# The inner layer of the compression on column strips: sixteen positions of a half go in turn to four strips of 32 columns

## The reference, cut to what matters

```python
def compress(kv, pos_emb, w1, b1, w2):       # kv: (1, 256, 2 groups, 128)
    n_cmp = (S - 32) // 16 + 1               # 15 windows
    idx = arange(n_cmp)[:, None] * 16 + arange(32)[None, :]
    blocks = kv[:, idx] + pos_emb            # (15 windows, 32 positions, 2 groups, 128)
    flat = blocks.reshape(n_cmp, G, 32 * 128)
    return silu(flat @ w1 + b1) @ w2         # w1: (4096, 128), w2: (128, 128)
```

## Time and profile before

| what | value |
|---|---|
| median of three runs | 2127.25 us |
| the profiled execution | 2127.4 us |
| its span on the core | 2125.6 us |
| TensorE matmul busy | 2095.3 us (99% of the span), 11559 records |
| TensorE weight loads busy | 1799.6 us (85%) |
| VectorE / ScalarE / GpSimd busy | 1413.3 / 1050.3 / 106.2 us |
| share of TensorE in the chain that ended last | 79% |
| mean granted TensorE clock | 0.999 |

### The profile page before, as it was taken

How to read it: one execution, slowest core, us unless ns; L and a number is a source line. 1 busy time by engine, 2 the same in 40 slices (tenths; PEclk the granted TensorE clock), 3 DMA queues, 4 the chain that set the end, 5 groups by cost and what they waited for, 6 DMA issues and landing times.

```text
span 2125.6 us, 27729 instructions
## 1 busy us (share of the span) xinstructions
PE 2095.3 (99%) x11559; PEld 1799.6 (85%) x11559; DVE 1413.3 (66%) x1802; ACT 1050.3 (49%) x1520; POOL 106.2 (5%) x121
## 2 busy tenths in 40 slices
PE   8999999999999999999999999999999999999998
PEld 7989888989888888887888888888888878888887
DVE  5657876657877766665675566675766667655655
ACT  5344646444645555545454454554544454444543
POOL 0100010010010010000000000000100000000000
PEclk9999999999999999999999999999999999999999
DMA  8353245453235665444554465565644545544552
GB/s 284 112 199 128 94 136 180 122 199 125 95 123 203 209 217 172 164 139 159 178 181 157 149 216 189 198 208 184 212 156 159 158 159 178 184 173 151 194 184 96
DMA packets 193271, 357.24 MB, mean 168 GB/s; under 512 B 8381, under 2 KB 85369, under 8 KB 193146
## 3 DMA queue, kind: packets, MB, share of 16 engines
q1 hardware_dynamic: 190410, 345.51, 48.7%
q0 software_dynamic: 2736, 9.96, 1.3%
HBM read 354.40 MB, written 1.05 MB: 167 GB/s over the span
## 4 chain that ended last, share of the span: by engine, by line
PE 79%; DVE 3%; ACT 1%; issue 0%; DMA 0%; POOL 0%; DVEq 0%; ACTq 0%
PE bank L2029 14%; PE bank L2033 14%; PE bank L2039 14%; PE bank L2071 12%; PE bank L2075 6%; PE bank L2093 2%; PE bank L2084 2%; PE bank L2053 2%; PE bank L2056 2%; PE bank L2059 2%; PE bank L2110 1%; PE bank L2213 1%; DVE raw_r L2538 1%; PE bank L2101 1%; PE bank L2296 1%; PE bank L2131 1%
## 5 line engine op out<-in xcount | busy, mean ns | idle before, releaser
L2538 DVE TENSOR_TENSOR raw_r<-raw,high 128x2048 fp32r<-128x2048 f32 x304 | 686.3, 2267 | 78.4 <-ACT high L2322 77.2
L2322 ACT ACTIVATE high<-raw 128x2048 fp32r<-128x2048 f32 x304 | 575.5, 1897 | 228.2 <-PE bank L2039 173.0
L2029 PE MATMUL bank<-high,units_r 128*128 128x512 f32 (+1 forms) x1576 | 628.8, 399 | 4.4 <-ACT high L2322 3.0
L2033 PE MATMUL bank<-high,units_r 128*128 128x512 f32 (+1 forms) x1576 | 615.3, 390 | 2.0 <-DVE units_r L2562 1.1
L2039 PE MATMUL bank<-raw_r,units_r 128*128 128x512 f32 (+1 forms) x1576 | 423.4, 389 | 0.0
L2029 PEld LDWEIGHTS bank<-high,units_r 128*128 128x128 f32 x1576 | 296.8, 188 | 65.5 <-issue 4.0
L2033 PEld LDWEIGHTS bank<-high,units_r 128*128 128x128 f32 x1576 | 297.0, 188 | 61.3 <-DVE units_r L2559 2.2
L2039 PEld LDWEIGHTS bank<-raw_r,units_r 128*128 128x128 f32 x1576 | 296.1, 188 | 62.3 <-DVE raw_r L2538 0.7
L2071 PE MATMUL bank<-units_r,high 128*128 128x512 f32 x1152 | 288.2, 392 | 0.0
L2071 PEld LDWEIGHTS bank<-units_r,high 128*128 128x128 f32 x1152 | 208.4, 189 | 38.1
L2075 PEld LDWEIGHTS bank<-units_r,raw_r 128*128 128x128 f32 x1152 | 157.2, 190 | 11.2
(11 more groups left out here) (262 smaller groups left out, 2207.2 us busy)
## 6 DMA issues: line engine op xcount, KB each, us to landing
raw<-in_ffn_w_dram SPq DMA_DIRECT2D x132, 1024.0 KB, 5.1
raw<-in_w_in_dram SPq DMA_DIRECT2D x108, 1024.0 KB, 5.1
raw<-in_w_out_dram SPq DMA_DIRECT2D x24, 1024.0 KB, 4.9
raw<-in_cross_wkv_dram SPq DMA_DIRECT2D x16, 1024.0 KB, 5.2
raw<-in_w_branch_dram SPq DMA_DIRECT2D x12, 1024.0 KB, 4.9
raw<-in_cross_wq_dram SPq DMA_DIRECT2D x8, 1024.0 KB, 5.4
raw<-in_cross_wo_dram SPq DMA_DIRECT2D x8, 1024.0 KB, 4.9
raw<-in_w_in_dram SPq DMA_DIRECT2D x4, 832.0 KB, 4.5
```

The costliest lines, as they stand in the source:

```text
L2029: pe.matmul(o, h.high(k0 + k)[:, span], p.hi[k][:, cols], start=start and k == 0, stop=False, skip_group_check=True)
L2033: pe.matmul(o, h.low(k0 + k)[:, span], p.hi[k][:, cols], start=False, stop=False, skip_group_check=True)
L2322: done = act.activation(high, raw, ACT.Copy)
L2538: done = dve.tensor_tensor(low, raw, high.bitcast(F32), ALU.subtract)
```

## The change

The rows of e4 are padded from 15 to 16 windows per group, so that one position has 32 columns; the padding is set to zero by a memset. The 16 matmuls of a half write in turn to PSUM partitions 0 to 31, 32 to 63, 64 to 95 and 96 to 127, so each of the four strips collects eight of the 32 positions. The copy out takes all 128 partitions, and the turn is no longer a transpose: it multiplies the copied tile with a constant `sum4` (128 x 32, ones where the row modulo 32 is the column), which turns and adds the four strips at once. The step's entry in `plan.work` falls from 16 x 512 to 16 x 170 per half.

```diff
+    put("sum4", (p % 32 == j)[:, 0:32])
...
-                e4 = e.ap[:, 0:960].rearrange("p (l g n) -> p l g n", l=32, g=2)
+                e4 = e.ap.rearrange("p (l g n) -> p l g n", l=32, g=2)
...
-                    plan.work += 16 * 512
+                    plan.work += 16 * 170
...
-                hb, hs = st(30), st(30)
+                hb, hs = st(32), st(32)
...
-                c = plan.copy(f"{C}.hp", [("cmp_1", C)], hp.ap[0:30, 0:P], b.ap[0:30, 0:P], "dve", hp.after)
+                c = plan.copy(f"{C}.hp", [("cmp_1", C)], hp.ap[:, 0:P], b.ap[:, 0:P], "dve", hp.after)
...
         for i in range(16):
-            product = pe.matmul(bank.ap[0:30, 0:P], e4[:, 16 * half + i, :, :].rearrange("p g n -> p (g n)"),
-                                p.raw[:, i * P:i * P + P], start=half + i == 0, stop=half + i == 16,
+            strip = i % 4 * 32
+            product = pe.matmul(bank.ap[strip:strip + 32, 0:P], e4[:, 16 * half + i, :, :].rearrange("p g n -> p (g n)"),
+                                p.raw[:, i * P:i * P + P], start=half == 0 and i < 4, stop=half == 1 and i >= 12,
                                 skip_group_check=True)
...
-        pe.transpose(bank.ap[:, 0:30], src[0:30, 0:P], ident[0:30, 0:30]).then_inc(
+        hold.wait_ge(*at(("const",)))
+        pe.matmul(bank.ap[:, 0:32], src[:, 0:P], m.cst("sum4"), start=True, stop=True, skip_group_check=True).then_inc(
...
-            product = pe.matmul(bank.ap[0:15, g * P:g * P + P], hs[:, g * 15:g * 15 + 15], p.raw, start=True, stop=True,
+            product = pe.matmul(bank.ap[0:15, g * P:g * P + P], hs[:, g * 16:g * 16 + 15], p.raw, start=True, stop=True,
...
+        dve.memset(e4[:, :, :, 15:16], 0.0)
...
-                done = dve.tensor_tensor(e4[:, 16 * half:16 * half + 16, g, :], blocks[:, :, half:half + 15],
+                done = dve.tensor_tensor(e4[:, 16 * half:16 * half + 16, g, 0:15], blocks[:, :, half:half + 15],
...
-        dve.tensor_scalar(hb, bank.ap[:, 0:30], bias, None, ALU.add).then_inc(*mark(s.vout, ("cmp_bias", name)))
+        dve.tensor_scalar(hb, bank.ap[:, 0:32], bias, None, ALU.add).then_inc(*mark(s.vout, ("cmp_bias", name)))
```

## The result

| | before | changed | ratio (95% interval) |
|---|---|---|---|
| median of four runs each | 2126.80 us | 2107.72 us | 0.9911 (0.9899 to 0.9924) |
| range of the runs | 2126.23 to 2131.13 | 2107.38 to 2108.62 | |
| the profiled execution / its span | 2127.4 / 2125.6 | 2107.87 / 2106.1 | |

The change takes 19 us off, 0.9%. The forecast was 2115.2 us with a range from 2109.0: the direction was right, the saving was over half as large again as said, and it lies outside the range. It is close to the rival called full overlap (2109.7).

The account below looks back on a forecast made before the run. TensorE, busy in 99% of the span, was taken as the bound. From 2127.4 us: compressions -13.6, turns +0.4, switches +0.65, waits for the w1 piece +0.35, together -12.2, giving 2115.2 us; range 2109 to 2128.5.

Parts of the forecast that it names:

- full overlap: Rival for the four compression stretches: all strips work at once, 0.0275 to 0.037 us a record, 2109.7 to 2111.5 us; chance 0.28.
- The second record of instruction i can't start until the first has left the strip, and instruction i+1 stands behind it.: Compression matmuls: only neighbouring instructions overlap, so 32 take 33 record times, 3.62 us for 7.03; 13.6 us saved in four.
- The Trainium skill's order rule: Compression matmuls: starts and ends strictly in program order, taken as speaking against reading the skill's 3.07x into this change.
- Bounds: One compression's 64 records: 7.03 us without overlap, 1.76 with four strips at once; a 32-column load estimated at some 27 ns.
- The switches, +0.65 us in eight: TensorE going from whole array to strips and back: between 0 and 1.3 us in all, the middle taken.
- The turn, +0.4: The turn as a two-record float32 product instead of one record: +0.1 us each, +0.4 in four.
- Small edits, nothing: Memsets, strided additions, copy out, bias with 32 columns and 16 KB more constants: no cost; without cover 0.6 us a layer.
- The wait for the second piece of w1: Between the halves of the values' compression TensorE waits for the load: 0.1 and 0.2 us, put down as +0.35 in all.
- pairs: Main case for the compressions: only an instruction's second record and the next one's first overlap, 3.62 us each, 2115.2 us; chance 0.42.
- VectorE's waits: Sign to look for: VectorE's four waits for the compression, 6.2 us each, fall to about 2.8 each.
- What would come late next: After the values' compression: next w_in piece ready 12 us before use, TensorE's 1.95 us wait for VectorE stays, saving kept.
- The clock, which was left out: Granted clock 1.00 in the compression stretches and TensorE busy on both sides, so no clock term was counted.

## Why the prediction was wrong

Step by step, as it was put:

- **"The second record of instruction i can't start until the first has left the strip, and instruction i+1 stands behind it."** This is the step that failed. The first half of the sentence holds; the second doesn't. Instruction i+1 goes to another strip's queue, and the row that would have priced it was not there. A compression took 1.88 us where 3.62 was said, without the waits for the piece. Four of them are 7.0 us. That this is nearly the whole miss of 7.5 us is in part luck: the waits for the piece were 2.6 us dearer than said, and turns, switches and start-up came out cheaper by 0.9, 0.65 and 1.4. I had taken the order in which records start in the trace of before as a rule of the engine; there all records of a stretch like this use the same columns, so that order could not show what other columns do. The runs for eight, six, four and two records in a row fix what holds instead: order of handing out, four places per strip.
- **The Trainium skill's order rule.** On that step I had leaned on "TensorE: Matmul & The Clock Gate", Part 3, Packing small matmuls, which says that matmuls start and end strictly in program order. The trace disagrees for column strips: with eight records in a row the ninth starts with the fifth, ahead of the sixth to the eighth, and in turn, where each float32 instruction is two records, four strips start at once and full overlap is nearly reached, 7.10 / 1.88 = 3.8x. Its 3.07x for four row tiles is lower than what column strips give here. The measurement decides.
- **Bounds.** The two ends, 1.76 and 7.03 us, were right, and nothing speaks against the estimate of 27 ns for a load of 32 columns: no load held up a matmul (64 records in 1.88 us are 29 ns each). The full overlap's end of the range was set at 2109 from 2109.7, without room for its own small terms being too dear: 1.05 us were put down for turns and switches, and they came to -0.5.
- **The switches, +0.65 us in eight.** Nothing. "The trace has no such switch" was a misreading: the kernel before pays on the way into these products and out of them, as much as the changed one. The way in, before and then after:

```profile
93.72 1.07 PE L2039 MATMUL bank<-raw_r,units_r 128*128 128x512 f32 x4
94.72 7.17 PE L2131 MATMUL bank<-raw,units 128*30 128x128 f32 x64
...
92.26 1.07 PE L2040 MATMUL bank<-raw_r,units_r 128*128 128x512 f32 x4
```

  It is 1.00 us from the first of four products to the compression in both (92.26 to 93.26 after), 0.09 more than to a turn from 128 partitions. On the way out, 7.10 - 64 x 0.109 = 0.12 us are left before and 1.88 - 16 x 0.109 = 0.14 after. "TensorEngine Tiling (Array Packing)", Key Properties, in the Trainium skill says that a change of mode drains TensorE. No run here shows whether the kernel before changes the mode for its 30 columns too; with the 1.3 us that I worked out for the rule the sum would have been 1.3 too high.
- **The turn, +0.4.** It is -0.5: 0.13 us each against 0.17 to the next start, and 0.09 less ahead of each. The rows of 15 x 15 and 128 x 15 were poor neighbours.
- **Small edits, nothing.** Right within the interval: 0.9997 (0.9988 to 1.0007) with all of them and no strips.
- **The wait for the second piece of w1.** The place was right, and its size under full overlap nearly: 1.7 to 2.3 us were said, 3.0 and 2.5 measured. Under pairs 0.35 was said.
- **VectorE's waits** for the compression fell from 24.7 to 7.3 us in four, 1.8 each; for pairs 2.8 were said.
- **What would come late next.** Nothing else did: the next w_in piece was in time, and the wait ahead of L2216 stayed (1.57 for 1.95). The clock, which was left out, has a stretch of 0.50 two microseconds behind the new wait in one of two profiled executions.

With the stretches, turns and waits as measured, the sum is 2127.4 - 18.4 = 2109.0; the profiled execution took 2107.9, and the difference is less than the 1.4 of the start-up, which varies between executions. The chance of 0.28 for full overlap was too low for a case against which no row with two strips spoke, only a rule.

## What to carry to other kernels

Small matmuls with at most 32 output partitions, each with its own stationary and summed anyway, can be dealt out to four strips of columns; visit the strips in turn or in blocks of at most four records (two float32 instructions), and sum the strips in a product that is there already. An order seen in a trace where everything shares one resource says nothing of work on different resources: leave that end of the range wide, or measure it by itself. When a stretch becomes four times shorter, look at once for the load that it covered, and give it time by moving work rather than by cutting the piece, since slots are counted in pieces.

## What was unexpected of the hardware

- A strip of 32 columns holds four records, one running and three waiting. The next strip's first record starts together with the fifth of eight (0.46 to 0.47 us after the first) and with the third of six (0.25 us); with four in a row there is no loss (1.96 against 1.88 us). What happens when the last instruction of a sum lies in a shorter queue than another was not tried.
- Records on different strips start within 20 ns for four. The time falls as the number of strips: 7.11, 3.62 and 1.88 us for one, two and four.
- A float32 product of two records from 128 partitions takes 0.13 us between weight products of the whole array, the same product from 64 partitions 0.33 and from 32 partitions 0.34. The products with fewer rows also start 0.09 us later behind the product ahead of them, and so do the compressions with 30 or 32 columns. Whether that is a change of mode was not measured by itself.
- The slow pace of TensorE at the start ends at 14 to 18 us, at another time in each execution. Later come stretches of 3.4 us at a granted clock of 0.50, none to two of them in an execution (three in the kernel with the piece cut in two, one of them twice as long), and one at the very end of each. But for these last, each one in the traces here begins in a wait of TensorE of 1.2 to 5.2 us or at most 2.1 us behind its end; most waits of 1.2 to 2.3 us have none. A stretch in which TensorE is busy costs an estimated 1.7 us, half of its 3.4.
